# Attention scores as two fp32r passes over rounded and remainder operands, with constant bf16 products ahead of each unit

## Chip, cores, metric

One core of one Trainium2 chip. The metric is device time of one launch in microseconds (us).

## What is computed

Two transformer blocks over x of 512 tokens by 1024. The first has a mixer with two kinds of attention (eight NSA heads, eight MoBA heads, head size 64) and a mixture of 32 experts; the second has a convolution, a forgetting attention of 16 heads and a retrieval of single experts (PEER). The change touches the attentions only. With the sizes of this case NSA selects every block, and both its selected and its window branch are causal attention over all 512 positions; MoBA is causal attention over all too. What is left of them, per head:

```python
s = jnp.einsum('bhqd,bhkd->bhqk', q, k) * scale
s = s - slope * (t[:, None] - pos[None, :])        # NSA and MoBA: a slope per head
s = s + c[..., :, None] - c[..., None, :]          # forgetting attention: a decay per head and position
p = softmax(where(pos <= t, s, NEG))               # causal
o = einsum('bhqk,bhkd->bhqd', p, v)
```

NSA heads have a third branch over 31 compressed keys, and add the three with gates.

## The kernel before

The kernel is one program of stages, each a block in which the five engines run their own instruction streams and meet through semaphores; a barrier stands between stages. `attention` is called twice: as `att1` by `nsa_and_moba` with 12 entries in `heads` (8 NSA heads, whose two units are the selected and the window branch of one query head; then 4 pairs of MoBA heads) and as `att2` with 8 pairs of forgetting heads.

Each entry has 8 units (`UNITS`): query tile t = 0 to 3 (128 queries), and u = 0, 1 for the two branches or the two heads of the pair. Unit g is `step(g)` = (head i, t, u), with n = g % 8. A unit looks at (t+1)*128 keys. It passes through the engines as follows.

- TensorE, `score(g)`: one f32 product of q (66 rows: 64 of the head and 2 more that carry slope or decay) with k into bank `sc[g % 2]`, then a bf16 product that adds the causal mask.
- VectorE, `maximum(g)`: the negated row maximum. ScalarE: the exponential into `prob[g % 2]`, with the row sum.
- TensorE, `turn(g)`: t+1 transposes of the probabilities into `pt`. VectorE, `move(g)`: copies them out.
- TensorE, `value(g)`: t+1 products with v into bank `o`. VectorE, `finish(i, n)`: scales and gates the result of a whole head, spread over the next head's units.

TensorE's order in step g is: `turn(g)`, `score(g+2)`, `value(g-1)`, then one `operand(i+1, n-1)` for n = 1 to 4, and for NSA heads `cmp_score` after unit 3 and `cmp_turn` after unit 6. `operand(i, m)` transposes q or k of the next head (4 transposes of 128x66) into the one bank `tq`; the rows come from `rows`, which GpSimd fills by copies (L946, L947). ScalarE copies `tq` out (`operand_out`, L1047). A pair has four operands, an NSA head one (q), but heads 0 and 4 have three, since k is shared by four NSA heads. For the first head of a stage each operand has a bank of its own, and all are transposed before the first score. VectorE's order in step g is: `move(g)`, `maximum(g+2)`, other stages' small pieces (`dve_between`), `finish(i-1, n)`; with n = 4 in NSA heads the mask and maximum of the compressed scores follow. ScalarE's is: exponential of g, `operand_out(i+1, n-2)`, other pieces (`act_between`, rounding weights of the next stage), for n = 5 the exponential of the compressed scores.

SP loads weights of later uses and fills a part of `y_rows` with zeros (L932).

## Time and profile before

| | |
|---|---|
| time before, median of 2 | 3520.71 us (3520.35 to 3521.07) |
| the profiled execution | 3518.24 us |
| its span | 3516.2 us |
| first attention | 207 to 388 us |
| second attention | 1952 to 2061 us |
| mean granted TensorE clock | 0.979 |

The span runs from the first instruction to the last; the execution's own time has 2 us around it. Engines: PE is TensorE's products and transposes, PEld its weight loads, DVE VectorE, ACT ScalarE, POOL GpSimd, SP the engine that issues DMAs. An f32 product shows as two records, a transpose, an fp32r product and a bf16 product as one.

### The profile page before, as it was taken

To read this page: it belongs to the slowest core of one execution; us is meant where nothing else is said; L and a number is where in the kernel's file an instruction comes from. 1 tells how busy PE (TensorE), PEld (TensorE's weight loads), DVE (VectorE), ACT (ScalarE), POOL (GpSimd) and SP (SyncE) were. 2 spreads that over 40 slices of the span, in tenths; PEclk is the share of its full clock that TensorE was granted. 3 is DMA by queue.
4 is the path that set the end of the run, shared out by engine and by line. 5 is a ranking of instruction groups with operands and counts; after the bars stand their busy time and mean duration, and the time that the engine had idled before them with its cause. 6 is when DMAs were issued, how large, how long until landed. Compare 5 with 4: busy or idle time off the path is not lost. (4 is left out here: it accounts for less than half of the span.)

```text
span 3516.2 us, 38763 instructions
## 1 busy us (share of the span) xinstructions
PE 3195.4 (91%) x13430; PEld 2169.4 (62%) x13430; DVE 2854.0 (81%) x4753; ACT 1431.9 (41%) x1763; POOL 735.7 (21%) x724
## 2 busy tenths in 40 slices
PE   7999979999999999999999999888888888888876
PEld 5878757777777777766787788544344434343432
DVE  6867679999999999967993554788888888888886
ACT  3235338888888888853233632111111111111110
POOL 0000021000000000010000100344444444444442
PEclk9999989999999999999999999999999999999999
DMA  7422269999999999974233024999999999999998
GB/s 264 165 85 103 74 232 391 405 406 402 405 405 401 406 407 402 409 272 146 92 101 120 25 84 169 407 417 421 420 409 415 418 411 404 421 418 406 421 414 347
DMA packets 251798, 1100.57 MB, mean 313 GB/s; under 512 B 21208, under 2 KB 30832, under 8 KB 185840
## 3 DMA queue, kind: packets, MB, share of 16 engines
q1 hardware_dynamic: 166221, 523.62, 39.1%
q0 software_dynamic: 79680, 558.14, 38.8%
q10 hardware_dynamic: 5760, 17.04, 1.2%
q8 instruction: 78, 1.28, 0.1%
q14 instruction: 59, 0.48, 0.0%
HBM read 1069.64 MB, written 33.03 MB: 314 GB/s over the span
## 5 line engine op out<-in xcount | busy, mean ns | idle before, releaser
L2148 DVE TENSOR_TENSOR moe_w_lo<-ring,moe_w_hi 128x2048 fp32r<-128x2048 f32 x384 | 860.6, 2282 | 27.6 <-ACT moe_w_hi L1996 26.6
L1996 ACT ACTIVATE moe_w_hi<-ring 128x2048 fp32r<-128x2048 f32 x380 | 720.9, 1915 | 160.7 <-DMA ring<-in_exp_w 145.7
L2937 PE MATMUL last_banks<-last_rows_b,ring 128*128 128x512 f32 x1024 | 501.7, 637 | 129.5 <-DVE ring L3137 129.1
L2937 PE MATMUL last_banks<-last_rows_a,ring 128*128 128x512 f32 x1024 | 475.5, 608 | 82.8 <-DVE ring L3137 82.2
L3029 ACT ACTIVATE last_gelu<-last_dot 128x2 f32<-128x2 f32 (+1 forms) x257 | 52.3, 203 | 1117.0 <-DVE last_dot L3134 1116.9
L2937 PEld LDWEIGHTS last_banks<-last_rows_b,ring 128*128 128x128 f32 x1024 | 198.5, 202 | 407.9 <-issue 210.7
L2937 PEld LDWEIGHTS last_banks<-last_rows_a,ring 128*128 128x128 f32 x1024 | 187.5, 192 | 326.0 <-issue 194.9
L2816 POOL DMA_INDIRECT last_rows_a<-in_peer_uv,last_ids x256 | 283.3, 1107 | 499.2 <-PE last_banks L2937 317.6
L2816 POOL DMA_INDIRECT last_rows_b<-in_peer_uv,last_ids x256 | 298.3, 1165 | 381.4 <-PE last_banks L2937 360.1
L3137 DVE TENSOR_SCALAR ring<-consts_sb,last_gelu,last_gates 128x128 f32<-128x128 f32 x512 | 162.0, 398 | 75.6 <-ACT last_gelu L3029 74.7
L1745 POOL COPY moe_col<-slots 128x1 uint32 (+1 forms) x30 | 34.9, 1164 | 858.5 <-PE moe_tp L1792 471.0
L3134 DVE CUSTOM_DVE_ANT_0 last_rows_b<-last_rows_b,ring 128x1024 f32<-128x1024 f32 x128 | 155.3, 1224 | 52.2 <-DMA last_rows_b<-in_peer_uv,last_ids 49.4
L3134 DVE CUSTOM_DVE_ANT_0 last_rows_b<-last_rows_b,last_h 128x1024 f32<-128x1024 f32 x128 | 154.5, 1223 | 38.3 <-DMA last_rows_b<-in_peer_uv,last_ids 35.1
L3134 DVE CUSTOM_DVE_ANT_0 last_rows_a<-last_rows_a,ring 128x1024 f32<-128x1024 f32 x128 | 154.2, 1223 | 33.4 <-DMA last_rows_a<-in_peer_uv,last_ids 32.2
L3134 DVE CUSTOM_DVE_ANT_0 last_rows_a<-last_rows_a,last_h 128x1024 f32<-128x1024 f32 x128 | 153.5, 1221 | 28.6 <-DMA last_rows_a<-in_peer_uv,last_ids 27.3
L2566 DVE SCALAR_TENSOR_TENSOR conv_rows<-glu,conv_taps,conv_rows 128x512 f32<-128x512 f32 x240 | 160.9, 743 | 0.5
L260 DVE TENSOR_TENSOR mix_lo<-ring,mix_hi 128x2048 fp32r<-128x2048 f32 (+1 forms) x48 | 107.2, 2245 | 57.4 <-ACT mix_hi L251 57.0
L251 ACT ACTIVATE mix_hi<-ring 128x2048 fp32r<-128x2048 f32 (+1 forms) x48 | 90.0, 1881 | 115.8 <-DMA ring<-in_w_in 52.2
L307 PE MATMUL conv_acc<-mix_hi,ht_hi 128*128 128x512 f32 x320 | 126.1, 394 | 0.0
L309 PE MATMUL conv_acc<-mix_hi,ht_lo 128*128 128x512 f32 x320 | 125.7, 393 | 0.0
L308 PE MATMUL conv_acc<-mix_lo,ht_hi 128*128 128x512 f32 x320 | 125.0, 391 | 0.0
L1083 DVE COPY spare<-att_pt 128x128 f32<-128x128 f32 (+3 forms) x160 | 78.2, 489 | 44.7 <-PE att_pt L975 41.1
(597 smaller groups left out, 6365.5 us busy)
## 6 DMA issues: line engine op xcount, KB each, us to landing
ring<-in_exp_w SPq DMA_DIRECT2D x384, 1024.0 KB, 11.4
ring<-in_w_in SPq DMA_DIRECT2D x38, 1024.0 KB, 5.6
ring<-in_ada_w SPq DMA_DIRECT2D x12, 1024.0 KB, 13.2
z<-in_ada_w SPq DMA_DIRECT2D x12, 1024.0 KB, 7.3
y_rows<-moe_y ACTq DMA_DIRECT2D x17, 512.0 KB, 6.8
ring<-in_w_out SPq DMA_DIRECT2D x8, 1024.0 KB, 5.1
y_rows<-spare SPq DMA_DIRECT2D x1, 7680.0 KB, 25.0
gate_rows<-conv_held ACTq DMA_DIRECT2D x4, 1024.0 KB, 8.2
```

The lines of the kernel that those rows point to most:

```text
L251: self.env.nc.scalar.activation(self.hi[:, m % RAW, 0:n], self.raw[:, i % RAW, 0:n], ACT.Copy).then_inc(self.hi_done, 1)
L260: self.env.nc.vector.tensor_tensor(self.lo[:, i % RAW, 0:n], self.raw[:, i % RAW, 0:n], self.hi[:, m % RAW, 0:n].bitcast(F32), ALU.subtrac ...
L307: nc.tensor.matmul(out, lhs[0], rhs[0], start=start, stop=False)
L308: nc.tensor.matmul(out, lhs[0], rhs[1], start=False, stop=False)
L309: return nc.tensor.matmul(out, lhs[1], rhs[0], start=False, stop=stop)
L1996: nc.scalar.activation(w_hi[:, slot, :], env.ring[:, slot, :], ACT.Copy).then_inc(hi_done, 1)
L2148: nc.vector.tensor_tensor(w_lo[:, slot, :], env.ring[:, slot, :], w_hi[:, slot, :].bitcast(F32), ALU.subtract).then_inc(lo_done, 1)
L2566: ins = nc.vector.scalar_tensor_tensor(conv[:, n, :], glu[:, n, tap:tap + S], taps[:, n, tap:tap + 1], conv[:, n, :], ALU.mult, ALU.add)
L2816: nc.gpsimd.indirect_dma_start(slot(n), None, d["peer_uv"], bass.IndirectOffsetOnAxis(ids[:, u % 4, s:s + 1], 0)).then_inc(gathered[n % SL ...
L2937: last = nc.tensor.matmul(sums(t)[:, q, :], diag[:, n % SL], slot(n)[:, D + q * W:D + (q + 1) * W], start=first, stop=final)
L3134: nc.vector.tensor_tensor_reduce(left, left, h(t), 1.0, 0.0, ALU.mult, ALU.add, dot[:, n % SL:n % SL + 1]).then_inc(dotted, 1)
L3137: nc.vector.tensor_scalar(diag[:, n % SL], ident, act_out[:, n % SL:n % SL + 1], gates[:, u % 4, n % K:n % K + 1], ALU.mult, ALU.mult).the ...
```

## The change

- Operands. q and k are turned straight from where they lie, without GpSimd's copies, 64 rows each. ScalarE copies `tq` as fp32r (rounded) into the lower 64 partitions of `qa` or `ka` and then copies that once more: q's into `qb`, k's into the upper half of `ka`. VectorE subtracts the rounded from the exact (`rest`): q's remainder goes into the upper half of `qa`, k's into `kb`.
- Scores. `score` makes two fp32r products over the same columns, `qa` (128 rows) with `ka` and `qb` (65 or 66 rows) with `kb`, where before there was one f32 product. The additional rows carry the slope and the position (written by GpSimd) or the decays (turned, copied and subtracted at the start of `att2`, then brought to their rows by four small DMAs per pair on SP's queue).
- Waits. `operand(i, m)` waits for the ScalarE copies and the subtraction of m-1; `score` and `cmp_turn` wait for the subtractions and second copies too. `operand(i+1, n-2)` now stands at the head of step n instead of at the end of step n-1.
- `warm`: four bf16 products of 128x128 constants ahead of `turn(g)`, where `cps` or a half of `o` is free.
- `move` of units n = 0 and 1 goes from VectorE to ScalarE (`move_act`).
- The compressed scores' decay is added by VectorE from a constant, not by two rows; their keys lie twice, one copy below the other.
- The zero fill is made first on GpSimd and its DMA stands ahead of the loads of w_out; ScalarE waits for it at unit 40.

```diff
-        qt, kt, prob, probt = part(0, 4), part(4, 4), part(8, 2), part(10, 2)
-        rows = sb("rows", [P, 4, NT, AUG])
+        prob, probt = part(8, 2), part(10, 2)
+        qa, ka, kb = (nc.alloc_sbuf_tensor_at(f"{name}_{n}", [P, 4, S], F32R, offset=spare_at + 4 * i * S) for n, i in (("qa", 0), ("ka", 4), ("kb", 12)))
+        qb = sb("qb", [P, 4, S], F32R)
+        low, high, aug_rows = slice(0, HD), slice(HD, P), slice(HD, HD + N_AUG)
+        by_act = lambda g: g % UNITS < ON_ACT
...
         def _(sp):
             if loads is not None:
-                loads(sp)
+                loads[0](sp)
+            if neg_c is not None:
+                sp.wait_ge(decay_hi, 1)
+                sp.wait_ge(decay_lo, 1)
+                for i, head in enumerate(heads):
+                    if i >= 2:
+                        sp.wait_ge(scored, UNITS * (i - 1))
+                    for u in range(2):
+                        for r in range(2):
+                            sp.dma_start(kb[HD + r:HD + r + 1, k_place(i, u), :].bitcast(F32), decay[head.decays[u]:head.decays[u] + 1, r, :].bitcast(F32)).then_inc(decay_landed[i % 2], 16)
...
         def _(pool):
+            if fill is not None:
+                nc.gpsimd.memset(zeros, 0.0).then_inc(zero_set, 1)
...
+                for n in range(4):
+                    for t in range(NT):
+                        if n + t:
+                            pool.wait_ge(aug_set, NT * n + t)
+                        nc.gpsimd.tensor_scalar(kb[aug_rows, n, t * P:(t + 1) * P], env.const("iota")[aug_rows], float(t * P), None, ALU.add).then_inc(aug_set, 1)
...
-                    nc.gpsimd.tensor_copy(rows[:, n % 4, :, 0:HD], src[:, :, col:col + HD]).then_inc(prep, 1)
-                    nc.gpsimd.tensor_copy(rows[:, n % 4, :, HD:AUG], aug).then_inc(prep, 1)
...
             def operand(i, m):
-                n = base[i] + m
-                pe.wait_ge(prep, 2 * n + 2)
+                kind, u = heads[i].operands[m]
+                src, col = (zq, heads[i].q[u]) if kind == "q" else (zk, heads[i].k[u])
                 if i:
                     pe.wait_ge(tq_moved, first_move(i, m))
+                    pe.wait_ge(tq_rest, base[i] + m)
+                    pe.wait_ge(hi_twice, base[i] + m)
                 for t in range(NT):
-                    last = nc.tensor.transpose(turn_bank(i, m)[0:AUG, t * P:(t + 1) * P], rows[:, n % 4, t, :], ident)
+                    last = nc.tensor.transpose(turn_bank(i, m)[low, t * P:(t + 1) * P], src[:, t, col:col + HD], ident)
                 last.then_inc(tq_turn, 1)
+            def warm(i, n):
+                if not heads[i].cmp and (i == 0 or n >= 2 or not heads[i - 1].cmp):
+                    bank = cps[:, 0:P]
+                    if n_cmp(i):
+                        pe.wait_ge(c_free, n_cmp(i))
+                elif n >= 6 and i:
+                    bank = o[:, (i + 1) % 2, 0].rearrange("p t e -> p (t e)")[:, 0:P]
+                    pe.wait_ge(o_free, i)
+                else:
+                    return
+                for _ in range(4):
+                    nc.tensor.matmul(bank, ident_b[:], causal_b[:], start=True, stop=True)
...
-                nc.tensor.matmul(sc[:, g % 2, 0:end], qt[0:AUG, q_place(i, u), t * P:end], kt[0:AUG, k_place(i, u), 0:end], start=True, stop=False)
+                nc.tensor.matmul(sc[:, g % 2, 0:end], qa[:, q_place(i, u), t * P:end], ka[:, k_place(i, u), 0:end], start=True, stop=False)
+                nc.tensor.matmul(sc[:, g % 2, 0:end], qb[0:HD + N_AUG, q_place(i, u), t * P:end], kb[0:HD + N_AUG, k_place(i, u), 0:end], start=False, stop=False)
...
             for g in range(STEPS):
                 i, n = g // UNITS, g % UNITS
+                if i + 1 < len(heads) and 2 <= n <= len(heads[i + 1].operands) + 1:
+                    operand(i + 1, n - 2)
+                warm(i, n)
                 turn(g)
...
-                if i + 1 < len(heads) and 1 <= n <= len(heads[i + 1].operands):
-                    operand(i + 1, n - 1)
...
-                dst = qt[0:AUG, q_place(i, u)] if kind == "q" else kt[0:AUG, k_place(i, u)]
-                nc.scalar.activation(dst, turn_bank(i, m)[0:AUG, :], ACT.Copy).then_inc(tq_moved, 1)
+                dst = qa[low, q_place(i, u)] if kind == "q" else ka[low, k_place(i, u)]
+                nc.scalar.activation(dst, turn_bank(i, m)[low], ACT.Copy).then_inc(tq_moved, 1)
+                act.wait_ge(tq_moved, first_move(i, m) + 1)
+                twice = qb[low, q_place(i, u)] if kind == "q" else ka[high, k_place(i, u)]
+                nc.scalar.activation(twice, dst.bitcast(F32), ACT.Copy).then_inc(hi_twice, 1)
...
+                if g and by_act(g - 1):
+                    move_act(g - 1)
                 if i + 1 < len(heads) and 2 <= n <= len(heads[i + 1].operands) + 1:
                     operand_out(i + 1, n - 2)
...
+            def rest(i, m):
+                kind, u = heads[i].operands[m]
+                dve.wait_ge(tq_moved, first_move(i, m) + 1)
+                if kind == "q":
+                    nc.vector.tensor_tensor(qa[high, q_place(i, u)], turn_bank(i, m)[low], qa[low, q_place(i, u)].bitcast(F32), ALU.subtract).then_inc(tq_rest, 1)
+                else:
+                    nc.vector.tensor_tensor(kb[low, k_place(i, u)], turn_bank(i, m)[low], ka[low, k_place(i, u)].bitcast(F32), ALU.subtract).then_inc(tq_rest, 1)
...
             for g in range(STEPS):
                 i, n = g // UNITS, g % UNITS
-                move(g)
+                if not by_act(g):
+                    move(g)
                 if g + 2 < STEPS:
                     maximum(g + 2)
+                if i + 1 < len(heads) and 2 <= n <= len(heads[i + 1].operands) + 1:
+                    rest(i + 1, n - 2)
                 if dve_between is not None:
                     dve_between(dve, g)
```

## Rows read from the trace of the kernel before

**Rows 1.** The page, busy us of each engine, share of the span, instructions

```profile
PE 3195.4 (91%) x13430; PEld 2169.4 (62%) x13430; DVE 2854.0 (81%) x4753; ACT 1431.9 (41%) x1763; POOL 735.7 (21%) x724
```

**Rows 2.** Windows: start:end, length, busy us of each engine (records), clock, DMA

```profile
core 0: us, PE busy (x) PEld busy (x) DVE busy (x) ACT busy (x) POOL busy (x), PEclk, DMA share, GB/s
207.40:388.30 180.90, 174.10 (x1278) 143.51 (x1278) 141.82 (x362) 86.33 (x252) 13.37 (x51) 1.00 0.23 86
1952.00:2060.80 108.80, 105.58 (x785) 86.55 (x786) 75.96 (x169) 62.33 (x174) 13.92 (x50) 1.00 0.01 1
```

**Rows 3.** Waits in the first attention: who waited for whom, us, times, longest

```profile
PE att_pt L975 <- ACT spare L1055: 4.5, 9, 0.7
ACT spare L1047 <- PE att_tq L958: 29.2, 22, 2.3
ACT att_cs L1063 <- DVE att_cs L1138: 16.7, 7, 2.9
```

**Rows 4.** Timeline of a pair head: start, us, engine, line, out<-in, records merged

```profile
344.89 0.39 PE L967 MATMUL att_sc<-spare 66*128 66x128 f32 x2
345.11 0.22 PE L968 MATMUL att_sc<-att_causal_b,att_ident_b 128*128 128x128 bf16 x1
345.17 1.05 PE L985 MATMUL att_o<-z,spare 128*128 128x64 f32 x8
...
348.40 0.60 PE L958 MATMUL att_tq<-consts_sb,att_rows 128*66 128x128 f32 x4
349.05 0.81 PE L967 MATMUL att_sc<-spare 66*128 66x384 f32 x2
350.62 0.59 ACT L1047 ACTIVATE spare<-att_tq 66x512 f32<-66x512 f32 x1
```

**Rows 5.** Windows of single heads: one NSA head, then two pair heads

```profile
219.30:234.80 15.50, 14.83 (x110) 12.26 (x108) 13.25 (x35) 6.08 (x21) 0.53 (x2) 1.00 0.21 68
1990.70:2004.20 13.50, 13.43 (x102) 10.98 (x102) 10.48 (x24) 8.93 (x25) 2.35 (x8) 1.00 0.00 0
2031.00:2044.20 13.20, 13.20 (x103) 11.02 (x101) 9.53 (x23) 6.85 (x21) 0.00 (x0) 1.00 0.00 1
```

**Rows 6.** Timelines: fp32r products of 512 columns, bf16 products of 94

```profile
1945.67 0.39 PE L308 MATMUL conv_acc<-mix_lo,ht_hi 128*128 128x512 f32 x1
1945.89 0.39 PE L309 MATMUL conv_acc<-mix_hi,ht_lo 128*128 128x512 f32 x1
475.27 0.70 PE L1449 MATMUL out_acc<-out_of_block,out_of_slot 128*128 128x94 bf16 x12 [0.21 <-DVEq L1635]
```

**Rows 7.** Timeline of the mask's end and maximum; a subtraction of the expert stage

```profile
349.70 0.22 PE L968 MATMUL att_sc<-att_causal_b,att_ident_b 128*128 128x128 bf16 x1
349.96 0.56 DVE L1077 TENSOR_REDUCE att_nmax<-att_sc 128x1 f32<-128x384 f32 x1 [0.21 <-PE att_sc L968]
L2137 DVE TENSOR_TENSOR moe_xt_lo_a<-moe_tp,moe_xt_hi_a x30: 677/681/685, 538.2 to 1463.4; 128x512 fp32r<-128x512 f32 x30
```

**Rows 8.** Timeline of the first attention's start; DMA issues, us to landing last

```profile
203.80 0.92 PE L958 MATMUL att_tq<-consts_sb,att_rows 128*66 128x128 f32 x4 [2.12 <-POOL att_rows L947]
204.63 0.94 POOL L939 MEMSET spare<- 128x1024 f32 x1
y_rows<-spare SPq DMA_DIRECT2D x1, 7680.0 KB, 25.0
out_rw<-in_router_w SPq DMA_DIRECT2D x1, 128.0 KB, 3.9
```

**Rows 9.** Windows and timeline of other stages where TensorE is half busy

```profile
456.60:460.00 3.40, 1.70 (x14) 1.46 (x14) 3.23 (x7) 1.71 (x3) 0.00 (x0) 1.00 1.03 423
460.00:463.40 3.40, 3.40 (x15) 2.80 (x14) 2.37 (x8) 0.65 (x1) 0.00 (x0) 0.50 1.02 412
457.57 1.10 PE L1360 MATMUL out_tp<-consts_sb,spare 128*128 128x128 f32 x8 [1.33 <-DVE spare L1555]
582.90:586.30 3.40, 1.76 (x8) 1.13 (x7) 3.40 (x2) 3.37 (x3) 0.00 (x0) 1.00 1.02 404
```

156 lines of the change are left out of this document (100 added, 56 removed).

## Prediction

> **What bounds the kernel now.** I read the busy shares first [rows 1]: TensorE is busy 91% of the span, but that covers five stages. The change touches two, the attentions, so I cut those out by time [rows 2]. From 207.4 to 388.3 us and from 1952.0 to 2060.8 us TensorE is busy 174.1 of 180.9 us and 105.6 of 108.8 us, at a granted clock of 1.00; VectorE is at 78% and 70%, ScalarE at 48% and 57%, DMA at 23% and 1%. The waits agree [rows 3]: in the first attention TensorE waits for ScalarE's exponentials 4.5 us in all, while ScalarE's operand copies wait 29.2 us for TensorE's transposes. So both stages go at TensorE's pace, 290 us of 3516 us. Nothing outside them changes in kind, and what they gain or lose moves the end one for one. The kernel's gain cannot be more than a few tens of us, whatever the change does.
>
> **TensorE's pace by piece.** Busy times overlap; what counts is start to start, from one head of the timeline [rows 4]. A 128x128 f32 transpose takes 0.11 us (four: (0.60-0.27)/3). A value product of 64 columns is two records, 0.22 us (eight records: (1.05-0.27)/7 each). A score product is two records as well: 0.22 us for 128 columns (344.89 to 345.11) and 0.65 for 384 (349.05 to 349.70) [rows 4, 7], so in proportion 0.44 for 256 and 0.86 for 512. The bf16 mask product takes 0.06 (345.11 to 345.17). A head of two units per query tile (a pair head) has 20 transposes, 20 values, 2 scores of each width, 8 masks and 16 operand transposes: 2.2+4.4+4.34+0.5+1.8 = 13.2 us. The rows of single heads say 13.5 and 13.2 [rows 5]. The pace model holds, with 0 to 0.3 us of waiting. The NSA heads take 15.5 us, of which some 0.7 us TensorE is idle [rows 5].
>
> **What the change takes off TensorE.** One f32 product becomes two fp32r products over the same columns. An fp32r product of 512 columns costs 0.22 to 0.23 us (1945.67 to 1945.89) [rows 6], so in proportion, and never under what a load of 128 weight columns seems to take (0.11 a record in the value products, of few columns), I take 0.23, 0.18, 0.13 and 0.12 for 512, 384, 256 and 128, each rounded up. Two passes: 0.46, 0.36, 0.26, 0.24 against 0.86, 0.65, 0.44, 0.22. Saved per head: 2 x (0.40+0.29+0.18-0.02) = 1.7 us, 34 us over 20 heads. Unknown is the narrow product: between a quarter of the 512 price, 0.06, and f32's own 0.22. With 80 such passes that is -5 to +8 us.
>
> **What it puts on TensorE.** Four bf16 products of 128 columns; 12 of 94 columns took 0.70 us, 0.045 each [rows 6], so about 0.06 each, 0.24 for four. They are placed in every unit of the eight pair heads of the second attention (64), in 30 units of the four pair heads of the first, in units 6 and 7 of NSA heads 1 to 7 (14): 108 x 0.24 = 26 us. They stand behind the operand's transposes and ahead of `turn`, whose exponential has mostly been there for long [rows 3], so they are on the path. A pair head's own TensorE work becomes 13.2-1.7+1.9 = 13.4 us: nothing gained.
>
> **The new wait, which decides.** There is one bank `tq` for the next head's operands. Before, `operand(m)` waited for one ScalarE copy of m-1. Now it waits also for `tq_rest`, the VectorE subtraction of m-1. VectorE's program has that subtraction behind `maximum(g+2)`, which waits for `score(g+2)`, which TensorE issues behind `operand(m-1)`, the four products and `turn(g)` of the same step. So two successive operands are a closed loop. From the end of operand m-1 at unit 2: products 0.24, turn 0.22, two passes of 384 columns 0.36, mask to its end 0.22, then to VectorE 0.04, maximum 0.56 less 0.08 overlap with the next, subtraction 0.68 (a TENSOR_TENSOR with the same fp32r output and a source in PSUM, 128x512) [rows 7], signal 0.05: 2.3 us, with the operand's own 0.44, 2.7 us a step. TensorE's own work in that step is 0.44+0.24+0.22+0.36+0.06+0.22 = 1.54. It stands 1.2 us. At unit 3 the values take 0.22 more, so it stands 1.0. At unit 4, with 512 columns, the step is 0.44+0.24+0.33+0.46+0.26+0.61+0.68+0.05 = 3.1 against 2.0 of work: 1.1. Together 3.3 us in each head whose next head has four operands. The 0.61 is the maximum of 512 columns, 0.56 x 4/3 less some fixed part and the overlap. VectorE's `move`, of the maximum's size, lies in the shadow of the scores, ScalarE's two copies (0.59 each [rows 4]) end before the subtraction. Behind the waiting transposes stand `turn` and `score`, so ScalarE and VectorE get nothing new either: no work fills the gap.
>
> ScalarE has a small stall of its own. At unit 5 it makes two copies (1.2) and an exponential of 512 columns, which I put at 0.7, against 1.7 of TensorE; some 0.2 us at unit 6. A head: 13.4+3.3+0.2 = 16.9, against 13.5 or 13.2 (of which up to 0.3 idle, gone into the new waits): +3.4.
>
> Sum. Second attention, 7 heads with a successor: +24. First attention, heads 8, 9, 10: +10. Head 7 (NSA, then four operands): -1.7+0.5+2.4 = +1 (its compressed scores, 0.9 us, fill the wait at unit 3). Head 3 (three operands): 0. The six other NSA heads: -1.7+0.2, and of that half a us stays with a chain that ScalarE waits for, `c_sub` behind VectorE's work at unit 4 (16.7 us in eight heads [rows 3]); I take -1.0 each: -6, with 0 and -9 as ends. The last head of each stage: 0. VectorE's load in these heads is up to 13.3 of 15.5 us [rows 5]; it loses two moves of 128 columns and gains one subtraction, +0.1: no new bound.
>
> The starts. Before the first score of the second attention now come a transpose of the decays, a ScalarE copy, a subtraction and four small DMAs of one row each, and beside them eight ScalarE operand copies instead of four. ScalarE has five copies more, 5 x 0.59 = 3.0 us; the first transposes no longer wait for GpSimd's two row copies (2.12 us of idle ended by them at the stage's start, of which the copies are some 0.5 [rows 8]): +2.5. The DMAs come last if they are slow: transpose 0.5, copy 0.6, subtraction 0.7, four issues, and the quickest small load took 3.9 to land [rows 8]; that is 6 to 8 us after the start against 6: up to +5. In the first attention ScalarE has three copies more (1.8), and GpSimd writes 16 short rows in turn after a 0.94 us fill [rows 8], each some 0.2 to 0.3: 4 to 6 us against some 4 before: +1.5. The filling DMA now leaves ahead of w_out, right after the start; it took 25 us [rows 8], and its first reader waits at unit 40, five heads or some 75 us on: hidden. Later decay DMAs have a head's 13 us: hidden. GpSimd loses its row copies, for which no TensorE wait stands in the loop [rows 3]: 0.
>
> 24+10+1+0-6+2.5+1.5 = +33 us. On the profiled span of 3516 us (that execution 3518.2; the median of the runs shown 3520.7, 2.5 above): 3554.
>
> **The rivals.** *A, the gain side: the subtraction is not felt.* If it ended before TensorE had done the step's other work, what stays is -34+26 us of work, +4 at the starts, some -1 elsewhere: 3515. For it: VectorE is only 70 to 78% busy. Against: the program order, which no share of busy time shows. It decides where the mean wait (35 of them, 36 us forecast) falls below 0.1 us. 0.12. *B, the clock falls.* Waiting 3.3 of 17 us thins TensorE's work. Before, both attentions held 1.00; but from 456.6 to 460.0 us TensorE was busy 1.70 of 3.40 us, eight of its 14 records transposes, and was granted 0.50 next, while 1.76 of 3.40 us of wide products kept 1.00 [rows 9]. The new steps are busy 1.5 of 2.7 us, half of it transposes. At 0.50 the pieces take twice as long (four transposes 0.92 for 0.60 at 203.8 [rows 8]); a third of 180 us at that level would cost half of it, 30 us: 3585. The bf16 products speak against it. 0.15. *C, VectorE and ScalarE block more than I sum.* VectorE's 10.5 us of a pair head that also splits weights [rows 5] become 10.5+2.7-0.6 = 12.6 of 16.9, bunched in the units where it is waited for, and ScalarE rounds weights in the same heads; another 0.6 us in each of 11 heads, and +5 at a start: 3565. 0.13. My forecast: 0.60.
>
> The Trainium skill, "TensorE: Matmul & The Clock Gate", Part 4, says that transposes in transpose mode do not count as work for the clock. By that rule rival B is likelier than a busy share lets one think and the time tends to 3585. This case's trace speaks both ways: the stretch at 456.6 agrees, the attentions, a third transposes and at 1.00 throughout, do not contradict it, since their f32 products were wide.
>
> **How the numbers follow.** The forecast's own range: the narrow product (-5, +8), NSA heads (-3, +6), starts (-1, +4), and a fifth of the 36 us of waits either way give 3540 to 3570. Leaving out A and the upper half of B, the range is 3530 to 3585. Two per cent, 70 us, is about what a measurement of this kernel can tell from no change. No case gains that; a clock at half for most of both attentions would lose it. Faster 0.01, same 0.95, slower 0.04.
>
> **What would show it.** In the profile after: pair heads of 16.9 us instead of 13.5; NSA heads of 14.5; the transposes of `operand` waiting for VectorE's subtraction about 1 us each at units 3, 4 and 5, 36 us in all, where before they waited for nobody; score products with 0.46 us for two passes of 512; eight copies on ScalarE before the first score of the second attention. Wrong would be: pair heads at 13.4 (A), a granted clock under 0.95 in an attention (B), or `turn` waiting for exponentials more than 10 us (C).

## The result and the profile after

| | before | after |
|---|---|---|
| time, median of 2 | 3520.71 us (3520.35 to 3521.07) | 3607.02 us (3599.95 to 3614.09) |
| the profiled execution, its span | 3518.24, 3516.2 us | 3599.95, 3598.1 us |
| mean granted TensorE clock | 0.979 | 0.972 |

The ratio is 1.0252, 95% interval 1.0235 to 1.0269: slower, and 22 us above the upper end of the forecast's range. The profiled span grew by 81.9 us, where the sum had 33.

The busy line stands against [rows 1]. TensorE is busy 20 us more, a quarter of the loss, and its share falls from 91 to 89%. So most of the loss is time in which TensorE waits, and its busy time also holds what the lower clock adds.

```profile
PE 3215.7 (89%) x13866; PEld 2200.5 (61%) x13866; DVE 2887.9 (80%) x4771; ACT 1482.1 (41%) x1864; POOL 733.8 (20%) x637
```

The windows of both attentions, of an NSA head and of two pair heads stand against [rows 2, 5]. TensorE was busy 174.1 of 180.9 us; now it is 181.84 of 209.4. The second attention went from 105.6 of 108.8 to 112.6 of 135.5. The granted clock of the first is 0.91, which was 1.00. The pair head of 13.5 us takes 17.2 us, of which TensorE is busy 13.9; ScalarE at 12.1 and VectorE at 11.4 are no bound either.

```profile
core 0: us, PE busy (x) PEld busy (x) DVE busy (x) ACT busy (x) POOL busy (x), PEclk, DMA share, GB/s
216.30:425.70 209.40, 181.84 (x1443) 161.11 (x1443) 152.02 (x354) 106.73 (x298) 21.98 (x15) 0.91 0.15 58
1996.70:2132.20 135.50, 112.58 (x1040) 100.43 (x1039) 89.05 (x178) 84.53 (x217) 0.00 (x0) 0.98 0.01 2
228.80:244.64 15.84, 13.54 (x115) 12.00 (x114) 13.47 (x34) 7.17 (x24) 1.48 (x1) 1.00 0.59 224
2031.20:2048.40 17.20, 13.91 (x134) 12.43 (x132) 11.39 (x23) 12.08 (x31) 0.00 (x0) 1.00 0.01 1
```

The waits from 2013.9 to 2117.4 us, six pair heads, name the one that the forecast put first: TensorE's operand transposes for VectorE's subtraction, three to a head, 18.7 us in 18 waits. The rows of before had no such wait [rows 3].

```profile
PE att_tq L990 <- DVE att_qa L1177: 12.9, 12, 1.2
PE att_tq L990 <- DVE att_kb L1179: 5.8, 6, 1.0
```

One turn of that loop in the timeline (start, us, engine, line, out<-in; in brackets the idle time and who ended it). The step from 2036.13 to 2039.01 is 2.88 us. Transposes, products, turn, score, maximum, subtraction and the next transposes follow each other as the forecast listed them.

```profile
2036.13 0.60 PE L990 MATMUL att_tq<-consts_sb,zq 128*64 128x128 f32 x4
2036.57 0.39 PE L1005 MATMUL att_cps<-att_causal_b,att_ident_b 128*128 128x128 bf16 x4
2036.79 0.39 PE L1035 MATMUL att_pt<-consts_sb,spare 128*128 128x128 f32 x2
2036.94 0.42 PE L1026 MATMUL att_sc<-att_ka,att_qa 128*128 128x384 f32 x1
2037.19 0.33 PE L1027 MATMUL att_sc<-att_kb,att_qb 66*128 66x384 f32 x1
2037.37 0.23 PE L1028 MATMUL att_sc<-att_causal_b,att_ident_b 128*128 128x128 bf16 x1
2037.64 0.56 DVE L1164 TENSOR_REDUCE att_nmax<-att_sc 128x1 f32<-128x384 f32 x1
2038.23 0.68 DVE L1177 TENSOR_TENSOR att_qa<-att_tq,att_qa 64x512 fp32r<-64x512 f32 x1
2039.01 0.60 PE L990 MATMUL att_tq<-consts_sb,zq 128*64 128x128 f32 x4 [1.19 <-DVE att_qa L1177]
```

The start of the first attention is where the sum was worst for its size [rows 8]. Every operand is ready at 207.8 us. GpSimd then still writes position rows until 214, in 16 instructions that start 0.60 us after each other (9.63/16), and behind them the first head's slope row of 1.5 us. The first score stands until 215.83.

```profile
204.47 9.63 POOL L967 TENSOR_SCALAR att_kb<-consts_sb 1x128 fp32r<-1x128 f32 x16
207.14 0.68 DVE L1179 TENSOR_TENSOR att_kb<-att_pt,att_ka 64x512 fp32r<-64x512 f32 x1 [0.59 <-ACT att_ka L1116]
214.18 1.50 POOL L976 TENSOR_SCALAR att_qb<-consts_sb 1x512 fp32r<-1x512 f32 x1
215.83 0.45 PE L1026 MATMUL att_sc<-att_ka,att_qa 128*128 128x128 f32 x1 [10.04 <-POOL att_qb L976]
```

In an NSA head with one operand, unit 3's transposes wait 0.93 us for an exponential. That exponential stands on ScalarE's queue behind the two copies, 0.59 and 0.63 us.

```profile
284.91 0.59 ACT L1116 ACTIVATE att_qa<-att_tq 64x512 fp32r<-64x512 f32 x1 [0.70 <-PE att_tq L990]
285.54 0.63 ACT L1119 ACTIVATE att_qb<-att_qa 64x512 fp32r<-64x512 f32 x1
286.07 0.45 ACT L1136 ACTIVATE spare<-att_sc,att_nmax 128x256 f32<-128x256 f32 x1
286.68 0.44 PE L1035 MATMUL att_pt<-consts_sb,spare 128*128 128x128 f32 x2 [0.93 <-ACT spare L1136]
```

At unit 6 of the same head the transposes wait 1.23 us for an exponential (first row), where before they waited 0.66 (second row, from the kernel before). The 0.57 us more and the 0.22 us of that unit's products make about the 0.77 us by which the head's last interval grew, 2.27 to 3.04. In the whole first attention `turn` waits 12.7 us for exponentials, in 16 waits, where [rows 3] has 4.5 in 9.

```profile
293.55 0.66 PE L1035 MATMUL att_pt<-consts_sb,spare 128*128 128x128 f32 x4 [1.23 <-ACT spare L1136]
296.30 0.66 PE L975 MATMUL att_pt<-consts_sb,spare 128*128 128x128 f32 x4 [0.66 <-ACT spare L1055]
PE att_pt L1035 <- ACT spare L1136: 12.7, 16, 1.4
```

And the clock. Windows of heads 6 and 7, in order (columns as above; the clock is the number ahead of the DMA share). TensorE is busy 1.96 of 3.40 us and is granted 0.52 next, the lower of its two levels (1.2 GHz); at 337.5 the same after 1.37 busy. Before, the window 310.3 to 313.7 was busy 3.15 of 3.40, and all of heads 6 and 7 ran at 1.00.

```profile
313.70:317.10 3.40, 3.40 (x31) 3.22 (x31) 1.10 (x4) 1.07 (x6) 0.00 (x0) 1.00 0.00 0
317.10:320.50 3.40, 1.96 (x17) 1.50 (x15) 3.02 (x11) 3.22 (x8) 0.00 (x0) 1.00 0.00 0
320.50:323.90 3.40, 3.40 (x18) 2.88 (x16) 2.48 (x7) 0.67 (x2) 0.00 (x0) 0.52 0.00 0
...
337.50:340.90 3.40, 1.37 (x13) 1.22 (x12) 3.06 (x10) 2.09 (x6) 0.00 (x0) 1.00 0.00 0
340.90:344.30 3.40, 3.40 (x20) 3.29 (x19) 2.02 (x4) 1.60 (x4) 0.00 (x0) 0.53 0.00 0
```

Two more stretches make up the 47.8 us at the lower clock. One, 208.0 to 221.6, begins in the idle time before the first score. The other, 361.6 to 371.8, lies in head 8, a pair head. Just ahead of that fall the bf16 products themselves waited: they are the first since the compressed branch of head 7 to write the bank `cps`, which VectorE still had to free (L1204). The wait ahead of the fall in head 7 was one for the subtraction, 2.03 us.

```profile
208.00:211.40 3.40, 0.00 (x0) 0.00 (x0) 0.00 (x0) 1.07 (x1) 2.90 (x7) 0.50 1.05 395
358.20:361.60 3.40, 2.23 (x22) 1.85 (x22) 1.54 (x6) 1.68 (x4) 0.00 (x0) 1.00 0.00 0
339.54 0.60 PE L990 MATMUL att_tq<-consts_sb,z 128*64 128x128 f32 x4 [2.03 <-DVE att_qa L1177]
361.31 0.40 PE L1005 MATMUL att_cps<-att_causal_b,att_ident_b 128*128 128x128 bf16 x4 [1.17 <-DVEq L1204]
```

**Where 81.9 us went.** From the two timelines, mask product to mask product of each head's first unit. The clock's part is an estimate: what heads 6 to 8 (18.7, 23.1, 24.2 us) take beyond the same units' full-clock intervals in neighbouring heads and runs (16.1, 18.8, 18.9).

| part | forecast | measured |
|---|---|---|
| start of the first attention | +1.5 | +8.2 |
| NSA heads 0 to 7, at full clock | -5 | +8 |
| pair heads 8, 9, 10, at full clock | +10 | +12 |
| heads 6 to 8, half clock | 0 | +12 |
| start of the second attention | +2.5 | +3.1 |
| pair heads of the second attention | +24 | +29 |
| outside both attentions, and between | 0 | +9 |

The last line is mostly 8.4 us of the last part, whose instructions are the same. Its length was 1457.6 us in the profile of before, 1458.8 in the kernel before with bf16 products, and 1461.6 to 1466.9 in all that hold the changed attention. The part between the attentions took 1563.5 us before, 1564.1 after, and up to 1577.9 in other profiles of this study, with instructions unchanged too. No run here says why; it stays open, and in every difference of whole times some microseconds are of this kind.

### The profile page after: what moved, and what is told of

Same layout as the page of the kernel before. It is cut to its first block and busy times, and to the rows that moved or that the text cites. A ratio compares the mean times of both kernels' runs of the same rounds, so it can differ in the third digit from the quotient of the medians.

```text
span 3598.1 us, 39808 instructions
## 1 busy us (share of the span) xinstructions
PE 3215.7 (89%) x13866; PEld 2200.5 (61%) x13866; DVE 2887.9 (80%) x4771; ACT 1482.1 (41%) x1864; POOL 733.8 (20%) x637
## 5 line engine op out<-in xcount | busy, mean ns | idle before, releaser
L3037 PE MATMUL last_banks<-last_rows_b,ring 128*128 128x512 f32 x1024 | 509.9, 645 | 128.2 <-DVE ring L3237 127.7
L3037 PEld LDWEIGHTS last_banks<-last_rows_b,ring 128*128 128x128 f32 x1024 | 200.6, 205 | 412.8 <-issue 214.1
L1164 DVE TENSOR_REDUCE att_nmax<-att_sc 128x1 f32<-128x128 f32 (+3 forms) x160 | 77.9, 487 | 47.7 <-PE att_sc L1028 47.6
## 6 DMA issues: line engine op xcount, KB each, us to landing
ring<-in_exp_w SPq DMA_DIRECT2D x384, 1024.0 KB, 11.4
```

The lines of the kernel that those rows point to most:

```text
L3037: last = nc.tensor.matmul(sums(t)[:, q, :], diag[:, n % SL], slot(n)[:, D + q * W:D + (q + 1) * W], start=first, stop=final)
```

## The experiments

"Length" is from the first instruction of a stage to the end of TensorE's last in it, "half" TensorE's time in it at the lower clock, summed from the trace's clock record. A "pair head" is one of the second attention between two others, an "NSA head" one whose successor has a single operand. A star marks one put together from undisturbed intervals of several heads, since the clock fell in each. Where full-clock heads differ, the table has the shortest (`five_two`, `five_none`). Lengths, halves and heads are those of the one profiled execution, the medians those of several: the profiled one took 3623.3 us in `aug_dve`, 3619.2 in `pool_copy` and 3618.3 in `act_moves`, above their medians, 3577.9 in `rest_first`, below it, and 3687.9 in `no_warm`. Ratios are to the kernel before on the same chip. `one_pass` leaves out one product of the scores; all others compute the whole.

| run | median us | ratio, 95% interval | att1 length, half | att2 length, half | pair head | NSA head |
|---|---|---|---|---|---|---|
| before | 3520.7 | 1 | 181.7, 3.4 | 110.2, 0 | 13.51 | 15.51 |
| after | 3607.0 | 1.0252 [1.0235, 1.0269] | 222.3, 47.8 | 142.3, 6.8 | 17.25 | 16.07 |
| after_again | 3611.6 | 1.0250 [1.0224, 1.0275] | 228.2, 61.4 | 142.4, 6.8 | 17.25 | 16.07 |
| no_warm | 3665.2 | 1.0382 [1.0317, 1.0447] | 255.2, 145.5 | 187.8, 163.8 | at half | 15.84 |
| rest_first | 3592.1 | 1.0200 [1.0176, 1.0225] | 210.4, 27.3 | 130.4, 6.8 | 15.61 | 16.06 |
| aug_dve | 3606.4 | 1.0234 [1.0210, 1.0258] | 231.0, 78.5 | 140.9, 3.4 | 17.27 | 16.07* |
| before_warm | 3547.0 | 1.0062 [1.0045, 1.0078] | 196.3, 13.7 | 123.2, 0 | 15.04 | 15.74 |
| warm_all | 3617.7 | 1.0270 [1.0253, 1.0287] | 224.3, 17.1 | 146.8, 6.8 | 17.86 | 17.21 |
| two_banks | 3586.9 | 1.0178 [1.0161, 1.0195] | 218.9, 17.1 | 127.8, 3.4 | 15.67 | 17.21 |
| pool_copy | 3605.9 | 1.0232 [1.0215, 1.0249] | 238.9, 88.7 | 141.0, 3.4 | 17.20 | 16.07 |
| all_three | 3576.3 | 1.0168 [1.0151, 1.0185] | 205.9, 3.4 | 127.8, 6.8 | 15.52 | 17.21 |
| act_moves | 3605.5 | 1.0248 [1.0231, 1.0265] | 238.8, 92.2 | 142.8, 6.8 | 17.34 | 15.41* |
| one_pass | 3597.5 | 1.0221 [1.0190, 1.0251] | 225.4, 81.9 | 135.8, 3.4 | 16.67 | 15.6* |
| all_five | 3557.4 | 1.0118 [1.0101, 1.0134] | 200.6, 10.2 | 119.8, 6.8 | 14.01 | 16.55 |
| two_products | 3626.0 | 1.0302 [1.0283, 1.0321] | 236.7, 88.7 | 146.1, 30.7 | 16.59 | 15.96* |
| five_two | 3557.1 | 1.0108 [1.0088, 1.0129] | 196.2, 13.7 | 116.0, 6.8 | 13.26 | 15.75 |
| five_none | 3554.1 | 1.0102 [1.0076, 1.0128] | 196.0, 34.1 | 115.2, 13.7 | 12.66 | 15.05 |

**The changed kernel again.**

> The changed kernel once more, unaltered. Its two runs lay 14 us apart and the last stage of its profile was 8 us longer than before, though the change does not touch that stage. Theory Q (queue order: the time goes into waits behind instructions in their engine's queue): the attentions' share of the loss repeats to a few us, heads with four operands to follow take 17.25 us again. Theory K (the clock: the time goes into half clock): the half-clock stretches in the first attention fall elsewhere and the total moves by 5 to 15 us with them. Last stage: if the 8 us are chance, this profile has it at 1450 to 1460 us; if they come from the change, at 1459 again.

The heads come out to the hundredth (17.25, 16.07). The clock does not: 61.4 us at half against 47.8. What falls to half clock varies between executions, so a whole time says little on a repair of a few microseconds; the heads at full clock say it.

**Without the bf16 products.**

```diff
             def warm(i, n):
+                return
```

> The four bf16 products ahead of each unit are left out, all else as in the changed kernel. Theory Q: they lie on the path in 108 units at 0.22 to 0.24 us, so about 24 us faster than the changed kernel (about 3580), pair heads 15.4 us, clock little changed. Theory K: without them the granted clock falls in more of both attentions; if half of the 290 us go at half clock, 50 us slower (about 3655), the mean clock in the attentions under 0.85.

It is slower than the changed kernel by 54 us, and the second attention ran at the lower clock for 163.8 of its 187.8 us. A pair head from 2060.0 takes 23.4 us, with a clock of 0.57:

```profile
2060.00:2083.40 23.40, 20.89 (x102) 18.44 (x101) 10.49 (x23) 11.90 (x30) 0.00 (x0) 0.57 0.01 1
```

So with the loop's waits in place the products hold the clock of that stage. The Trainium skill, "TensorE: Matmul & The Clock Gate", Part 4, says that transposes in transpose mode do not count as TensorE work for the clock. This run agrees with that, since its transposes did not keep the clock; the kernel before, with as many transposes, held 1.00, so the rule alone does not foretell the fall.

**The subtraction ahead of the maximum.**

```diff
+                if i + 1 < len(heads) and 2 <= n <= len(heads[i + 1].operands) + 1:
+                    rest(i + 1, n - 2)
                 if g + 2 < STEPS:
                     maximum(g + 2)
-                if i + 1 < len(heads) and 2 <= n <= len(heads[i + 1].operands) + 1:
-                    rest(i + 1, n - 2)
```

> One edit to the changed kernel: VectorE makes the subtraction of an operand ahead of the maximum of the same step, not behind it. Theory Q: the subtraction then waits only for ScalarE's copy, the next transposes stand some 0.4 us instead of 1.1, three times a head: pair heads 15.0 to 15.3 us instead of 17.25, 20 us over ten heads, and with less standing fewer half-clock stretches in heads 7 and 8 (up to 10 us more): 3575 to 3585. Theory K alone (the loop costs little): within 5 us of the changed kernel.

The pair head falls by 1.64 us, to a little above the 15.0 to 15.3 expected, the whole by 20 against the changed kernel on the same chip. In the timeline the wait of 1.19 is 0.70; the chain is now `turn`, VectorE's `move` (the copy below), subtraction, next transposes, which does not hang on the score.

```profile
2042.71 0.42 DVE L1170 COPY spare<-att_pt 128x256 f32<-128x256 f32 x1 [0.65 <-PE att_pt L1035]
2043.17 0.68 DVE L1177 TENSOR_TENSOR att_qa<-att_tq,att_qa 64x512 fp32r<-64x512 f32 x1
2043.95 0.60 PE L990 MATMUL att_tq<-consts_sb,zq 128*64 128x128 f32 x4 [0.70 <-DVE att_qa L1177]
```

The order on VectorE is thus shown to cost 1.64 of the 3.74 us that a pair head lost.

**Position rows by VectorE.**

```diff
+            if neg_c is None:
+                for t in range(NT):
+                    nc.vector.tensor_scalar(kb[aug_rows, :, t * P:(t + 1) * P], env.const("iota")[aug_rows].unsqueeze(1).to_broadcast([N_AUG, 4, P]), float(t * P), None, ALU.add).then_inc(aug_set, 1)
```

> One edit to the changed kernel: the position rows of the first attention are written by VectorE in 4 instructions of 512 elements instead of by GpSimd in 16 of 128, which took 9.6 us before the first score. Theory Q: the first score comes at about 208.5 instead of 215.8 us, 6 to 8 us faster as a whole, nothing else changed. If the start were hidden by something else (DMA, the table load of ScalarE): no change.

The first mask product comes 6.2 us after the stage's first instruction, where it was 12.9: 6.6 us of the start are shown to be GpSimd's. Two rows:

```profile
207.26 2.62 DVE L1214 TENSOR_SCALAR att_kb<-consts_sb 1x512 fp32r<-1x512 f32 x4
212.12 0.30 PE L1020 MATMUL att_sc<-att_ka,att_qa 128*128 128x128 f32 x1 [3.62 <-DVE att_kb L1173]
```

The median gained 5 us. In the profiled execution, the longest of the five, the first attention spent 78.5 us at half clock; what the clock took from the others, no trace shows. The Trainium skill, "GPSIMD Engine Reference", section 3.1, says that a GpSimd instruction passes through two software dispatch hops where VectorE's has one; it has no figure for them. The rows agree in kind: one of 128 elements took 0.52 us and one of 512 took 1.48, so by a straight line, an estimate, 0.2 us of each short one is not elements, and 0.08 us more passes before the next of the chain starts.

**The kernel before with the products alone.**

```diff
+                warm(i, n)
                 turn(g)
```

> The kernel before, with the changed kernel's four bf16 products alone, in the same 108 units. They measure the price of those products where TensorE is the bound and at full clock throughout: 108 x 0.22 = 24 us by theory Q, so 3545, pair heads 15.3 instead of 13.5 us. If they fall into waits of TensorE instead: under 5 us.

This prices one half of the change by itself. A pair head takes 15.0 for 13.5 and TensorE is busy all of it; the second attention is 13.0 us longer, the whole 23 us. The forecast's 26 us for 108 units was right. The first attention spent 13.7 us at half clock, in heads 6 to 8. One of the two stretches, 340.7 to 344.1, came right behind a wait of the products for the bank `cps` (second row); the other, 306.5 to 316.8, came behind a wait of 0.51 us that the kernel before has too and kept its clock through.

```profile
2015.30:2030.30 15.00, 15.00 (x134) 12.79 (x132) 10.81 (x24) 8.90 (x26) 2.37 (x8) 1.00 0.00 1
340.43 0.41 PE L973 MATMUL att_cps<-att_causal_b,att_ident_b 128*128 128x128 bf16 x4 [1.25 <-DVEq L1123]
```

**The products in every unit, then a second bank.** `warm_all` puts them in 156 of the 160 units, all whose step makes a score, in the score's own bank and behind `turn`. `two_banks` adds to it that operands 1 and 3 of a pair head after a pair head go to `cps`.

```diff
+        two = lambda i: i > 0 and not heads[i].cmp and not heads[i - 1].cmp
-        turn_bank = lambda i, m: tq[:] if i else (tq[:], pt[:, 0, :], pt[:, 1, :], cps[:])[m]
+        turn_bank = lambda i, m: (cps[:] if m % 2 and two(i) else tq[:]) if i else (tq[:], pt[:, 0, :], pt[:, 1, :], cps[:])[m]
```

> The changed kernel with the four bf16 products in every unit (158, not 108) and placed between a unit's transposes and the next scores, into the score bank that is about to be written. Theory K (the clock in the first attention falls because its NSA heads have no such products in six units of eight): half-clock time in the first attention falls from 48 to 79 us to under 15, and the time by 10 to 25 us although 50 x 0.22 = 11 us of products are added: 3585 to 3600. Theory Q: clock aside, 5 to 11 us slower in the NSA heads, pair heads 17.25 as before, since the products move within the closed loop.

> As warm_all, but operands m = 1 and 3 of a pair head that follows a pair head are turned into the bank cps, so each operand waits for the subtraction of the one two before it, not of the one just before. Theory Q: the loop over one bank is open, the transposes wait at most 0.2 us: pair heads 14.0 to 14.5 us instead of 17.25, 3 us x 9 heads = 27 us faster than warm_all. If ScalarE or VectorE are the true bound of these heads: over 16 us.

The clock is better in `warm_all` (17.1 us at half), but NSA heads pay 1.14 us, a pair head takes 17.86 where 17.25 was expected (why, no run shows), and the whole is 6 us above the changed kernel on another chip: the 3585 to 3600 expected did not come. The second bank takes 2.2 us off a pair head, which stays well above the 14.0 to 14.5 expected; what was left is found in `all_five`. Either repair of the loop, the order or the bank, brings it to 15.6: the closed loop over one bank is shown from two sides.

**The second copy on GpSimd, then more moves on ScalarE.** In `pool_copy` GpSimd makes the copies of L1119. `act_moves` has `ON_ACT` = 4 besides.

> The changed kernel with the second copy of each operand (SBUF to SBUF, 0.63 us) on GpSimd instead of ScalarE. Theory Q: in NSA heads the exponential of unit 3 stands behind two copies and TensorE waits 1.1 us for it; with one copy 0.4 us: NSA heads 15.4 instead of 16.07, 5 us over eight heads. Pair heads: their operands also wait for the second copy; if GpSimd takes under 1 us for it nothing changes there, if it takes 1.5 us as its short rows did, pair heads become longer than 17.25. Against theory Q in the NSA heads: no change of the wait at unit 3.

> The changed kernel with the second operand copy on GpSimd and with the moves of units 0 to 3 of each head on ScalarE (0 and 1 before). It asks what holds the single-operand heads at 16.07 us. Theory (VectorE, nearly without a gap from unit 2 to unit 7, is their bound once ScalarE's copy is away): two moves of 0.3 to 0.5 us leave VectorE, the waits that came back at units 6 and 7 (2.31 and 3.04 us between masks) shrink by about 0.8 us together, and such a head takes 15.2 to 15.4 us. Pair heads: the operand's loop stays (VectorE loses work ahead of its subtraction, ScalarE gets some ahead of its copy), 17.0 to 17.6. Rival (the chain of the compressed branch is bound by its own steps, not by VectorE's load, or ScalarE takes its place): the single heads stay at 16.0 or grow. Whole: theory 3595 to 3603 at a clock like that of the run with the copy on GpSimd, rival 3606 or more.

In an NSA head of `pool_copy` unit 3 waits 0.26 us instead of 0.93 (first row), but unit 5, which had waited for nothing, now waits 0.51, and unit 6 as before 1.25, behind the compressed scores' chain. The intervals between masks go from 2.01 and 1.65 to 1.35 and 2.31: 0.66 us gained and given back, and the head stays at 16.07.

```profile
292.98 0.44 PE L1046 MATMUL att_pt<-consts_sb,spare 128*128 128x128 f32 x2 [0.26 <-ACT spare L1144]
297.30 0.55 PE L1046 MATMUL att_pt<-consts_sb,spare 128*128 128x128 f32 x3 [0.51 <-ACT spare L1144]
300.52 0.66 PE L1046 MATMUL att_pt<-consts_sb,spare 128*128 128x128 f32 x4 [1.25 <-ACT spare L1144]
```

With two moves fewer on VectorE, `act_moves` keeps both at 1.35 and 1.65, and a head at full clock is 15.41. So two things held these heads in a row, ScalarE's second copy and VectorE's load; taking the first alone gave nothing, both gave 0.66 us. `all_five` against `all_three` shows the same 0.66 on whole heads (17.21 to 16.55). The longer last interval, 3.04 us, stayed in both; no run takes it apart. Neither made the kernel clearly faster: the ratios, 1.0232 and 1.0248, stand against 1.0250, and both profiled executions, some 13 us above their medians, had 88.7 and 92.2 us of the first attention at half clock.

**One score pass.** The second product (L1027) is left out.

> The changed kernel with the second score product (Q's rounded part against K's remainder, with the position and decay rows) left out: the scores lack that part, all operands are still made and waited for. It asks what TensorE's second pass is worth where. Theory (in the units with an operand the bank's loop is the bound, elsewhere the unit's own chain, of which the pass is a link): at units 2 to 5 of a pair head nothing changes, at the four others 0.1 to 0.25 us each goes, so a pair head takes 16.4 to 16.8 us in place of 17.25, a single-operand head 15.2 to 15.6 in place of 16.0, and the two attentions together some 14 us less if the clock stays. Rival (TensorE's work is nowhere the bound in the changed kernel): heads stay within 0.15 us. Rival of the clock (less work on TensorE, more time at half clock): half-clock time of the first attention above the 48 and 61 us of the two runs of the changed kernel and of the second above 20, and the whole not faster than 3607.

A pair head falls by 0.58 us: 0.11 to 0.17 in each of its first four intervals, 0.02 to 0.08 in the next three, which have the operands and where the loop is the bound; the last grows by 0.11. An NSA head falls by some 0.46. The second attention is 6.5 us shorter. The first is not (225.4 us against 222.3 and 228.2), with 81.9 us at half: what less work on TensorE gains in its heads went with the clock. The whole is 3597.5, and the interval of its ratio overlaps those of the changed kernel.

**Three repairs, then five.** `all_three` is `two_banks`, the subtraction ahead of the maximum, and VectorE's position rows. `all_five` adds GpSimd's copies and `ON_ACT` = 4.

> The changed kernel with the three repairs that runs here have priced one at a time, put together: operands 1 and 3 of pair heads that follow pair heads go to the free bank cps (with the bf16 products in the score's own bank, in all units), VectorE's remainder subtraction stands ahead of the maximum, and VectorE writes the position rows of the first attention. Theory (the bank's loop sets the pair heads, GpSimd's rows the start): pair heads of the second attention fall below the 15.67 us of the run with two banks, to about 15.0, since the loop over each bank is 1.2 us shorter again in its wait behind the maximum; the first score comes about 6.5 us earlier than in the changed kernel; whole: 3587 less 6.5 less some 8 to 10, 3565 to 3575, if the clock stays as in the run with two banks (some 17 us at half in the first attention). It stays above the kernel before. Rival (with two banks the subtraction's place no longer matters, the units are bound by TensorE's and ScalarE's own work): pair heads stay at 15.5 to 15.7 and the whole is 3578 to 3584. Rival of the clock: the start gains 6.5 us and half-clock time of the first attention rises to 60 us and more, so that the whole is above 3585.

> The run with three repairs, and besides the second operand copy on GpSimd and the moves of units 0 to 3 on ScalarE. Theory: the pair heads gain from a ScalarE that has one copy of 0.6 us less in each operand unit and pay for two moves of 0.4 to 0.5 us each: 14.6 to 15.2 us; the single heads lose the wait at unit 3 and part of that at unit 6: 15.6 to 16.2 with the products in the score's bank (17.21 in the run with them in all units). Whole 3550 to 3568, still above the kernel before by 1%. Rival (moves on ScalarE delay the exponentials of units 2 to 5 by as much as VectorE gains): equal to the run with three repairs within 6 us.

`all_three` takes 3576.3 us, between theory and rival; its heads go by the rival: with a second bank the subtraction's place brings 0.15 us a pair head, not 0.7. The start gives its 6.6 us and this time the clock stays (3.4 us at half). `all_five` is where ScalarE's relief tells in the pair heads: 15.52 to 14.01 us, where 14.6 to 15.2 was expected. From 1989 to 2073 us TensorE waits for nothing in it.

**Fewer products.** `two_products` is the changed kernel with two in place of four; `five_two` and `five_none` are `all_five` with two and none.

> The changed kernel with two bf16 products in place of four in each of the 108 units. Theory (the products lie on the path of the units with an operand and of those without, 0.055 us each): 0.11 us less in each of 108 units, 12 us in all where the clock is full, so that a pair head of the second attention takes 16.4 to 16.6 us in place of 17.25. The clock: between the changed kernel (47.8 and 61.4 us at half in the first attention, 6.8 in the second) and the one without products (145.5 and 163.8); if it goes in proportion, the whole comes out at 3615 to 3640. Rival (the waits, not the lack of these products, set the clock; or two are enough): half-clock time as with four, and the whole 3595 to 3602.

> The version with the five repairs (two banks, subtraction ahead of the maximum, position rows by VectorE, second copy on GpSimd, moves of four units on ScalarE) and two bf16 products in each of the 158 units in place of four. Theory (waits gone, the clock holds with fewer products; each product is on the path at 0.055 us): pair heads 13.1 to 13.4 us in place of 14.0, single heads 16.0 to 16.3 in place of 16.55, the two attentions together 15 us less, the whole 3540 to 3548 if half-clock time stays under 20 us in the first attention. Rival (the clock hangs on these products): half-clock time of the first attention above 60 us and the whole above 3560.

> The version with the five repairs and no bf16 products. Theory (waits gone, the f32 value products and transposes alone hold the clock, as in the kernel before): pair heads about 12.6 us, under the 13.2 to 13.5 of the kernel before, the whole 3525 to 3535, which would show that the two-pass form itself is worth something once its operands cost no wait. Rival (the two-pass form thins TensorE's work so that the clock falls without the products): half-clock time above 60 us in each attention, pair heads of 17 us and more there, the whole 3575 to 3620.

With the waits in place two products are too few: 88.7 and 30.7 us at half, 3626 us, though a full-clock pair head is 0.66 us shorter. With the five repairs the number hardly matters for the whole: 3557, 3557 and 3554 us for four, two and none. The shortest pair head goes 14.01, 13.26, 12.66, and the half-clock time of the first attention 10.2, 13.7, 34.1 us. Those shortest heads answer to what I expected, but with fewer products they are not the rule: the pair heads at full clock run from 13.26 to 14.15 us in `five_two` and, five of them, from 12.66 to 13.72 in `five_none`. The whole times are some 10 and 20 us above the forecasts. Of `five_none`'s excess 13 us are the unchanged parts between and behind the attentions (1570.1 and 1464.2 us, against the profile of before); for the rest there are its 48 us at half clock and the longer heads. Two heads of `five_none`, one at each level of clock, against [rows 5], then one of the longer ones at full clock:

```profile
1990.80:2003.40 12.60, 12.18 (x102) 10.50 (x100) 9.12 (x20) 9.90 (x28) 2.42 (x4) 1.00 0.01 2
2017.00:2033.50 16.50, 15.55 (x102) 13.50 (x101) 11.95 (x24) 10.14 (x28) 2.57 (x4) 0.79 0.01 2
2033.51:2047.23 13.72, 12.46 (x102) 10.60 (x101) 11.85 (x24) 9.80 (x28) 2.43 (x4) 1.00 0.01 1
```

In that longer head the waits have come back. The next head's first score needs the last subtraction, which stands behind other work in VectorE's queue, and TensorE idles 0.68 us; the same stands at 2016.77 and 2033.26. The trace puts the wait down to no engine ("issue"), but the score starts 0.10 us after the subtraction's end.

```profile
2046.21 0.67 DVE L1177 TENSOR_TENSOR att_kb<-att_cps,att_ka 64x512 fp32r<-64x512 f32 x1
2046.98 0.30 PE L1028 MATMUL att_sc<-att_ka,att_qa 128*128 128x128 f32 x1 [0.68 <-issue]
```

At best, at full clock and without waits, the two passes are worth 0.85 us of a pair head's 13.51 and 0.45 of an NSA head's 15.51; in the longer heads they are worth nothing. No version with them beat the kernel before: the best is 1.0% above it.

## Why the prediction was wrong, step by step

The forecast was 3554 us with a range to 3585. The mechanism it called decisive was there, and the price of the products was right. Terms of the sum were wrong: the saving on the scores and the start were mis-sized, the NSA heads had the wrong sign, and the clock, put at nothing in the sum, took its share beside the forecast instead of in its place.

**The closed loop: right.** Forecast: steps of 2.7, 2.7 and 3.1 us, waits of 1.2, 1.0 and 1.1, a pair head of 16.9. Measured: 2.88, 2.89, 3.10; 1.19, 0.96, 0.97; 17.25. `rest_first` and `two_banks` each took its cause away and got 1.64 and 2.19 us a head back. Rival A, that it is not felt, is out.

**The products: right.** 0.22 us for four (2036.57 to 2036.79) where 0.24 stood, and +23 us in `before_warm` where 26 stood.

**"Saved per head: 1.7 us": too much.** From first pass to mask the timeline has 0.43 us for 384 columns (2036.94 to 2037.37), where I had 0.36, 0.54 for 512 (2042.81 to 2043.35) against 0.46, 0.33 for 256 (2035.51 to 2035.84) against 0.26, and 0.26 for 128 (2032.49 to 2032.75) against 0.24. I had rounded the fp32r price in proportion to the columns; each pass has a part that does not shrink with them. The saving against the f32 pieces is 2 x (0.32+0.22+0.11-0.04) = 1.2 us a head, 24 us over 20 heads in place of 34. `five_none`, with 0.85 us left in its best head at full clock, goes with the smaller size. Over the seven heads this is up to 3.4 of the 5 us by which the pair heads of the second attention were missed.

**"NSA heads -1.0 each": wrong in sign.** I let them gain by TensorE's work, although [rows 5] showed TensorE idle 0.7 us and VectorE at 13.3 of 15.5. They are held by a chain through VectorE and ScalarE, in which the second copy (0.63 us) and the subtraction (0.68 us) came to lie ahead of exponentials. The step said "VectorE's load: +0.1, no new bound" and looked at the load, not at the place in the queue. Some 0.66 us of each such head is shown by `act_moves` to be that queue; the longer last interval, +0.77, is the products and a longer wait behind the compressed scores' chain, and was not taken apart. The term was missed by 13 us. `pool_copy` shows how such a wait comes back at the next step when one link is taken out.

**"Each some 0.2 to 0.3": the term that GpSimd's 16 rows got.** No row of before showed that instruction, and the nearest shown, a fill of 128x1024 in 0.94 us, says nothing of a short row. The upper bound should have come from how one short instruction behaves, times 16, since they stand in a chain: at 0.6 us each the start is +8, not +1.5. `aug_dve` shows it with 6.6 us back.

**Rival B, the clock: held in part.** It was to take a third of both attentions at half and stand instead of the forecast. Its sign, a clock under 0.95 in an attention, came: 0.91 in the first. Of the 47.8 us there 34 lay in heads 6 to 8 and took some 12 us of time, a third and not the half that I reckoned; the row at 203.8, 0.92 for 0.60, did not show pieces of twice the length either. The second attention had 6.8 us, at its start. I had looked for the fall in the pair heads' loop, busy 1.5 of 2.7 us; the products hold the clock there. It fell in heads 6 and 7, NSA heads without products in units 0 to 5, behind waits of 1.44 us for an exponential (the row below) and of 2.03 for the subtraction, and in head 8 behind the products' own wait for `cps`, which the forecast did not have. `warm_all`, with products there too, had 17.1 us at half; `all_three`, with the waits shortened as well, 3.4. `before_warm` had 13.7 us in the same heads without the first two of these waits, so they are no full explanation. Why these heads fall, and not others, stays open, and which head falls differs from one execution to the next.

```profile
319.33 0.44 PE L1035 MATMUL att_pt<-consts_sb,spare 128*128 128x128 f32 x2 [1.44 <-ACT spare L1136]
```

**Rival C: partly.** Its sign came: `turn` waits for exponentials 12.7 us in the first attention, over the 10 named. But 12.2 of them are in the NSA heads, most of which C did not price, and a pair head was 0.35 us over the forecast, not 0.6. "+5 at a start" came as +8.2, from GpSimd's chain.

**The range.** Its four terms add up to 3538 to 3579, where the text has 3540 to 3570. It gave the starts (-1, +4) and the NSA heads (-3, +6). Measured were +7 and +13 beyond their terms, and the clock's 12 and the last part's 8 came on top, all in one direction. `after_again` repeats the loop, the start and the NSA heads to the hundredth or near it, so these misses are not chance; the clock's share is larger there (61.4 us at half), and why the last part is longer stays open.

## To carry to other kernels

Before a sum over instructions, find the bank or buffer that successive steps share, and write its loop out with each engine's queue order: here that step was right to 2%, while heads costed by TensorE's load alone came out with the wrong sign. Count a one-row instruction by what one costs on its engine, not by its elements, above all when it is one of a chain. This kernel, which put waits in the place of work, lost its clock elsewhere than where the waits per head are largest. Its constant products bought time back only while the waits were there, and could wait for a bank themselves, so first take away the waits. And when one engine's work shrinks, look for the next in its place: without the products some heads stood behind VectorE again.

## What was not expected of the hardware

- GpSimd wrote one row of 128 fp32r values in 0.52 us, 0.60 from one to the next in a chain, and one of 512 in 1.48; VectorE wrote a row of 512 in 0.66 (2.62/4).
- The same kernel spent 47.8 and 61.4 us of one stage at the lower clock in two executions. The same start, 6.6 us shorter, stood ahead of 78.5 us at half in `aug_dve` and of 3.4 in `all_three`.
- Four bf16 products of 128x128 took 0.22 us, and without them a stage with waits ran 163.8 of 187.8 us at the lower clock.
- Two fp32r passes took 0.26, 0.33, 0.43 and 0.54 us for 128, 256, 384 and 512 columns: a fourfold width costs twice the time.
